# First attention of a four-mixer transformer step: scores to scaled rows one step further ahead, and the compressed branch's probabilities and V stacked over rows for one-pass products

## The reference, cut to what matters

```python
p_cmp = masked_softmax(jnp.einsum('bghtd,bngd->bghtn', qg, k_cmp), cmp_end[None, :] <= t[:, None])
o_cmp = jnp.einsum('bghtn,bngd->btghd', p_cmp.astype(v_cmp.dtype), v_cmp)
...
o = g_blk[..., 0:1] * o_cmp + g_blk[..., 1:2] * o_sel + g_blk[..., 2:3] * o_win
...
return o @ w_out
```

## Time and profile before

| | |
|---|---|
| median of 3 runs | 2051.27 us (2050.69 to 2051.84) |
| the profiled execution's own time | 2049.75 us |
| its span, first to last instruction | 2047.9 us |
| TensorE matmuls busy | 1899.2 us (93%), x8988 |
| VectorE busy | 897.6 us (44%), x1324 |
| ScalarE busy | 742.0 us (36%), x1190 |
| GpSimd busy | 820.9 us (40%), x413 |
| mean granted clock of TensorE | 0.969 |
| chain that ended last, by engine | PE 79%, DVE 9%, POOL 4%, ACT 4%, issue 4% |

### The profile page before, as it was taken

How to read it: one execution, slowest core, us unless ns; L and a number is a source line. 1 busy time by engine, 2 the same in 40 slices (tenths; PEclk the granted TensorE clock), 3 DMA queues, 4 the chain that set the end, 5 groups by cost and what they waited for, 6 DMA issues and landing times.

```text
span 2047.9 us, 24253 instructions
## 1 busy us (share of the span) xinstructions
PE 1899.2 (93%) x8988; PEld 1530.5 (75%) x8988; DVE 897.6 (44%) x1324; ACT 742.0 (36%) x1190; POOL 820.9 (40%) x413
## 2 busy tenths in 40 slices
PE   5999999899899999998999969999898999999986
PEld 3786767688788888877677448878786888888865
DVE  5136786601458824863731451126465431032116
ACT  5346776342333222223233332224322432133232
POOL 3244666363034454445233044350033344434431
PEclk9999999999999999999999779999998999999988
DMA  4321000242022233233122002320021222222221
GB/s 146 116 100 41 1 1 29 85 155 103 1 93 99 96 123 120 85 107 123 58 85 99 21 0 82 103 96 8 11 103 64 100 98 91 98 103 85 100 103 41
DMA packets 24116, 162.43 MB, mean 79 GB/s; under 512 B 2800, under 2 KB 3312, under 8 KB 4976
## 3 DMA queue, kind: packets, MB, share of 16 engines
q1 hardware_dynamic: 23040, 159.39, 22.0%
q10 hardware_dynamic: 1008, 2.12, 0.3%
HBM read 159.40 MB, written 2.10 MB: 79 GB/s over the span
## 4 chain that ended last, share of the span: by engine, by line
PE 79%; DVE 9%; POOL 4%; ACT 4%; issue 4%; DMA 0%; DVEq 0%; SPq 0%; ACTq 0%; POOLq 0%
PE psum L451 76%; POOL w_lo L2206 2%; PE psum L753 2%; ACT w_hi_r L1033 1%; POOL q_st L2242 1%; DVE tmp L1644 1%; DVE sqt L1995 1%; ACT spare L1442 1%; DVE tmp L1852 1%; DVE tmp L2158 1%; DMA ring<-in_panels 0%; DVE acc L2003 0%; DVE negmax L2050 0%; DVE h_lo L1800 0%; DVE xt L1603 0%
## 5 line engine op out<-in xcount | busy, mean ns | idle before, releaser
L2206 POOL TENSOR_TENSOR w_lo<-ring,w_hi_r 128x2048 fp32r<-128x2048 f32 x142 | 657.4, 4631 | 989.8 <-ACT w_hi_r L1033 989.7
L451 PE MATMUL psum<-big_r,w_hi_r 128*128 128x512 f32 (+1 forms) x1568 | 479.1, 389 | 33.0 <-DVE big_r L1582 8.7
L451 PE MATMUL psum<-h_hi,w_hi_r 128*128 128x512 f32 x1200 | 473.3, 394 | 20.5 <-POOL w_lo L2206 11.5
L451 PE MATMUL psum<-h_lo,w_hi_r 128*128 128x512 f32 x1200 | 469.7, 391 | 0.0
L451 PE MATMUL psum<-h_hi,w_lo 128*128 128x512 f32 x1200 | 469.4, 391 | 0.0
L1033 ACT CAST w_hi_r<-ring 128x2048 fp32r<-128x2048 f32 x144 | 274.1, 1904 | 285.6 <-PE psum L451 282.8
L451 PEld LDWEIGHTS psum<-big_r,w_hi_r 128*128 128x128 f32 x1568 | 296.9, 193 | 95.0 <-issue 32.9
L451 PE MATMUL psum<-big_r,w_lo 128*128 128x512 f32 (+1 forms) x784 | 303.5, 387 | 0.0
L451 PEld LDWEIGHTS psum<-h_hi,w_hi_r 128*128 128x128 f32 x1200 | 227.0, 189 | 74.4 <-issue 14.4
L451 PEld LDWEIGHTS psum<-h_hi,w_lo 128*128 128x128 f32 x1200 | 226.8, 189 | 47.8
L451 PEld LDWEIGHTS psum<-h_lo,w_hi_r 128*128 128x128 f32 x1200 | 227.2, 189 | 47.2 <-issue 0.5
(11 more groups left out here) (305 smaller groups left out, 2327.0 us busy)
## 6 DMA issues: line engine op xcount, KB each, us to landing
ring<-in_panels SPq DMA_DIRECT2D x148, 1024.0 KB, 4.7
xt<-in_x SPq DMA_DIRECT2D x4, 512.0 KB, 6.5
out<-big SPq DMA_DIRECT2D x8, 256.0 KB, 2.2
big<-in_mem ACTq DMA_DIRECT2D x1, 1024.0 KB, 4.6
q_st<-in_ple ACTq DMA_DIRECT2D x1, 512.0 KB, 3.4
spare<-in_w_gate ACTq DMA_DIRECT2D x1, 192.0 KB, 6.4
spare<-in_w_k ACTq DMA_DIRECT2D x1, 128.0 KB, 8.8
params<-in_params ACTq DMA_DIRECT2D x1, 114.0 KB, 4.9
```

Of the source, the lines that this page charges most:

```text
L451: return nc.tensor.matmul(o, l, r, start=start, stop=stop, **kw)
L2206: g.tensor_tensor(w_lo[:, p], ring[:, p], plain(w_hi[:, p]), ALU.subtract).then_inc(lo_done[j], 1)
```

## The change

Two things change, both in the first attention.

1. `LEAD = 4`: in step k TensorE makes the scores of part k+4, VectorE the maximum of part k+4, ScalarE exp of part k+3, VectorE its coefficient and GpSimd its scaled rows. The steps begin at -4. Transposes, high and low halves, products and joins keep their step. Buffers keep their number (4 PSUM banks for scores, 4 in `q_st`).
2. CMP's product becomes one fp32r product over 63 rows. Rows 0 to 30 of `nsa_cmp` hold the high half of the transposed probabilities (ScalarE), rows 32 to 62 the low half (VectorE, in `nsa_low`). `vcmp` holds high and low V side by side (128 columns a group), the same in rows 0 to 30 and 32 to 62. Row 31 is zero from a memset. `vcmp` moves to `rstd`, `nsa_cmp` stays in `tmp`, both through fp32r twins. CMP's shifted scores go to `hid` instead of `q_st`, so that ScalarE's exp and not VectorE's subtraction waits for the old transposes. Transposes of part w now wait for the low half of part w-2 in every case.

```diff
-        STEPS = range(-3, max(products_at) + 2)
+        LEAD = 4
+        STEPS = range(-LEAD, max(products_at) + 2)
...
                 if w >= 2:
-                    if parts[w - 2]["br"] == CMP:
-                        pe.wait_ge(ns["hi"], w - 1)
-                    else:
-                        pe.wait_ge(ns["lo"], parts[w - 2]["lows"])
+                    pe.wait_ge(ns["lo"], w - 1)
...
                 if x["br"] == CMP:
-                    pe.wait_ge(ns["hi"], x["end"] + 1)
-                    last = mm(psum[0:HD, 6 + x["u"] % 2, :], vcmp[:, x["g"] * HD:(x["g"] + 1) * HD],
-                              nsa_cmp[x["u"] % 2], False, False)
+                    rows = HALF_ROWS + NCMP
+                    pe.wait_ge(ns["lo"], x["end"] + 1)
+                    last = mm(o, vcmp[0:rows, x["g"] * P:(x["g"] + 1) * P], nsa_cmp[x["u"] % 2][0:rows], False, False)
...
-                if 0 <= k + 3 < NW:
-                    nsa_score(parts[k + 3])
+                if 0 <= k + LEAD < NW:
+                    nsa_score(parts[k + LEAD])
...
-            nc.scalar.copy(vcmp[:, :], psum[0:NCMP, 1, 0:G * HD]).then_inc(evac[1], 1)
+            act.wait_ge(ns["zero"], 1)
+            for row in (0, HALF_ROWS):
+                last = nc.scalar.copy(nsa_cmp_values(row, 0),
+                                      psum[0:NCMP, 1, 0:G * HD].rearrange("p (g d) -> p g d", d=HD))
+            last.then_inc(ns["kv_hi"], 1)
...
+                if w >= 4:
+                    act.wait_ge(ns["turned"], w - 3)
                 if part["br"] == CMP:
-                    last = nc.scalar.activation(p, p, ACT.Exp)
+                    last = nc.scalar.activation(p, nsa_shifted(part), ACT.Exp)
...
-                if 0 <= k + 2 < NW:
-                    nsa_exp(parts[k + 2])
-                    if k + 2 == NW - 1:
+                if 0 <= k + LEAD - 1 < NW:
+                    nsa_exp(parts[k + LEAD - 1])
+                    if k + LEAD - 1 == NW - 1:
                         act.dma_start(mem_raw, a["mem"]).then_inc(mem_in, 16)
...
+            V.memset(plain(tmp_tw[:, :]), 0.0)
+            V.memset(plain(rstd_tw[:, :]), 0.0).then_inc(ns["zero"], 1)
...
+            kv += 1
+            dve.wait_ge(ns["kv_hi"], kv)
+            for row in (0, HALF_ROWS):
+                last = V.tensor_tensor(nsa_cmp_values(row, 1),
+                                       psum[0:NCMP, 1, 0:G * HD].rearrange("p (g d) -> p g d", d=HD),
+                                       nsa_cmp_values(0, 0, raw=True), ALU.subtract)
+            last.then_inc(evac[1], 1)
...
+                if part["br"] == CMP:
+                    x = nsa_cmp[part["u"] % 2]
+                    V.tensor_tensor(x[HALF_ROWS:HALF_ROWS + NCMP], psum[0:NCMP, 4 + w % 2, :], plain(x[0:NCMP]),
+                                    ALU.subtract).then_inc(ns["lo"], 1)
+                    return
...
-                    if w >= 4:
-                        dve.wait_ge(ns["turned"], w - 3)
-                    ins = V.tensor_tensor(nsa_probs(part).rearrange("p (x k) -> p x k", k=nk), s_,
+                    ins = V.tensor_tensor(nsa_shifted(part).rearrange("p (x k) -> p x k", k=nk), s_,
...
-                if 0 <= k - 1 < NW and parts[k - 1]["br"] != CMP:
+                if 0 <= k - 1 < NW:
                     nsa_low(parts[k - 1])
-                if 0 <= k + 3 < NW:
-                    nsa_max(parts[k + 3])
-                if 0 <= k + 2 < NW:
-                    nsa_coef(parts[k + 2])
+                if 0 <= k + LEAD < NW:
+                    nsa_max(parts[k + LEAD])
+                if 0 <= k + LEAD - 1 < NW:
+                    nsa_coef(parts[k + LEAD - 1])
...
-                if 0 <= k + 2 < NW:
-                    nsa_scale(parts[k + 2])
+                if 0 <= k + LEAD - 1 < NW:
+                    nsa_scale(parts[k + LEAD - 1])
```

More of the change, by code:

```diff
@@ L151, in nsa_schedule @@
             sums.append(dict(unit, br=br, first=br == SEL, last=br == WIN, blocks=blocks_, end=len(parts) - 1))
[L152 to L155, removed]
     at = {}
@@ L220, in program @@
         sqt = sb("sqt", [P, S])
-        rstd = sb("rstd", [P, S])
+        rstd, rstd_tw = sb("rstd", [P, S], twin=True)
         r_row = rstd
         gains = sb("gains", [P, 2 * KD])
-        tmp = sb("tmp", [P, 2 * S])
+        tmp, tmp_tw = sb("tmp", [P, 2 * S], twin=True)
         o_acc = sb("o_acc", [P, 2 * S])
@@ L229, in program @@
         kcmp = sb("kcmp", [P, CMPW])
-        vcmp = sb("vcmp", [NCMP, G * HD])
         spare, spare_r = sb("spare", [P, 8 * S], twin=True)
@@ L348, in nsa_probs, with nsa_shifted @@
             return q_st[:, n:n + part["nh"] * part["nk"]]
+        def nsa_shifted(part):
+            return hid[:, part["u"] % 4 * CMPW:(part["u"] % 4 + 1) * CMPW]
         def small(buf, part):
@@ L353, in small, with nsa_cmp_values @@
             return buf[:, n:n + part["nh"]]
-        nsa_cmp = [view("nsa_cmp", [NCMP, S], tmp, n * S) for n in range(2)]
+        HALF_ROWS = 32
+        vcmp = rstd_tw
+        nsa_cmp = [view("nsa_cmp", [P, S], tmp_tw, n * S) for n in range(2)]
+        def nsa_cmp_values(row, low, raw=False):
+            x = vcmp[row:row + NCMP]
+            return (plain(x) if raw else x).rearrange("p (g r d) -> p g r d", r=2, d=HD)[:, :, low, :]
         nsa_corr = [view("nsa_corr", [HD, S], buf) for buf in (acc, sqt)]
@@ L391, in program @@
         ns = {n: sem("nsa_" + n) for n in (
-            "kv_hi", "gates", "scores", "negmax", "probs", "coef", "scaled", "turned", "hi", "lo", "summed", "corr",
+            "kv_hi", "zero", "gates", "scores", "negmax", "probs", "coef", "scaled", "turned", "hi", "lo", "summed", "corr",
             "o", "o_hi", "o_lo")}
@@ L762, in nsa_product @@
                 if x["br"] == CMP:
-                    pe.wait_ge(ns["hi"], x["end"] + 1)
-                    last = mm(psum[0:HD, 6 + x["u"] % 2, :], vcmp[:, x["g"] * HD:(x["g"] + 1) * HD],
-                              nsa_cmp[x["u"] % 2], False, False)
+                    rows = HALF_ROWS + NCMP
+                    pe.wait_ge(ns["lo"], x["end"] + 1)
+                    last = mm(o, vcmp[0:rows, x["g"] * P:(x["g"] + 1) * P], nsa_cmp[x["u"] % 2][0:rows], False, False)
                 else:
                     if kt == 0:
-                        pe.wait_ge(ns["lo"], parts[x["end"]]["lows"])
+                        pe.wait_ge(ns["lo"], x["end"] + 1)
                     v = nsa_value(kt, x["br"], x["g"])
@@ L1239, in nsa_exp @@
                 p = nsa_probs(part)
+                if w >= 4:
+                    act.wait_ge(ns["turned"], w - 3)
                 if part["br"] == CMP:
-                    last = nc.scalar.activation(p, p, ACT.Exp)
+                    last = nc.scalar.activation(p, nsa_shifted(part), ACT.Exp)
                 else:
-                    if w >= 4:
-                        act.wait_ge(ns["turned"], w - 3)
                     s_ = nsa_scores(part)
@@ L1258, in nsa_hi @@
                 if part["br"] == CMP:
-                    ins = nc.scalar.copy(nsa_cmp[part["u"] % 2], psum[0:NCMP, 4 + w % 2, :])
+                    ins = nc.scalar.copy(nsa_cmp[part["u"] % 2][0:NCMP], psum[0:NCMP, 4 + w % 2, :])
                 else:
```

## The result

| | before | after |
|---|---|---|
| median of 6 runs each | 2050.98 us (2046.11 to 2051.94) | 2031.93 us (2027.29 to 2035.58) |
| ratio | | 0.9907 [0.9895, 0.992] |
| profiled execution, own time | 2049.75 us | 2029.03 us |
| its span | 2047.9 us | 2027.3 us |
| first attention, first scores to output projection | 166.01 to 347.75 = 181.74 us | 165.81 to 330.88 = 165.07 us |

The change was also timed twice more beside the kernel before, on other occasions: 2032.55 against 2049.37, and 2034.63 against 2050.3, so 16.8 and 15.7 us. The stage gives 16.67 us of this, and it does so in every profile of the change (165.07, 165.07 and 165.06 us).

A forecast was written before the change was run, and what follows sets the result against it. The prediction took TensorE to bound the kernel, with VectorE the nearest other engine. Its terms, 11.9 + 5.1 - 1.0 + 0.9 + 1.6 = 18.5 us, came off 2051.27 to give 2032.8 us, range 2027.7 to 2040.5.

The forecast's parts named there:

- product, 14 in the middle: Compressed products outside the tail: one fp32r product takes 0.48 us where 1.33 was, saving 14 x 0.85 = 11.9 us.
- lookahead, middle: Between head and tail: LEAD 4 removes 5.1 of 6.9 us of TensorE's waits for GpSimd's scaled rows; bounds 0 and 6.9.
- VectorE's 16 low halves: Compressed parts: the new low halves on VectorE mostly fall where it waits, costing 1.0 us; bounds 0 and 9.8.
- head: Start of the first attention: compressed scores fill TensorE's 3.09 us wait for the first scaled rows, gaining 0.9 us.
- tail: From the transposes at 341.17 to the output projection: 1.6 us saved of 6.58, bounds 0.5 and 1.9.
- Hence no term for it: Compressed product: its weight load runs beside the matmul ahead, so nothing was charged for it.
- the weight load of the new product is not hidden: Rival at the compressed product: 16 x 0.19 = 3.0 us lost again, 2035.8 us; chance 0.07.
- a VectorE wait at the change to the second pair of heads: Where the second pair of heads begins: TensorE still waits 1.8 us for VectorE's low half, taken off the lookahead's 6.9.
- my two cases: Head: clock falls as before, 0.9 us gained; or stays at 2.4 GHz, 3.2 gained, a rival of 2030.5 us, chance 0.30.
- The fall is seen once: Head: the clock fell once, after 3.1 us of idle, and stayed at 1.00 after weight-load idles of 1.1 and 1.6.
- One step ahead, these are gone before: Tail: with the lookahead, the last exponentials are done before ScalarE copies part 101; part of the 1.6 us saving.
- Preparation: Ahead of the attention: two memsets (1.5 us) and the V halves vanish in VectorE's idle time; cost zero.

The follow-up runs named there:

- e1: The change with the old plain fp32 compressed product, so only the lookahead of four steps is new against the kernel before; 2034.87 us, ratio 0.9928.
- e3: The change with the compressed product over all 128 rows in place of 63, the added rows zero; 2031.88 us, ratio 0.9912 against the kernel before.
- e4: The change with VectorE's compressed low half made twice, the second into rows the product does not read; 2037.84 us.
- e7: e3 plus eight fill matmuls in TensorE's idle 1.8 us ahead of the first compressed scores; 2030.14 us, ratio 0.9904 against the kernel before.
- e2: The change with LEAD set back to 3, so only the new compressed product is new against the kernel before; 2039.98 us, ratio 0.9949.
- e8: The change as it is, timed again beside e7 on the same chip; 2032.55 us, ratio 0.9912 against the kernel before.
- e10: The change as it is, timed again beside e9; 2034.63 us, ratio 0.9921 against the kernel before.
- e9: e7 plus ScalarE's copy of part 100 moved ahead of the last exponentials in the tail; 2028.49 us, ratio 0.9892 against the kernel before.
- e5: The change with the compressed product over 64 rows, and again over 96, in place of 63; 2030.92 us with 64, 2031.59 us with 96.

## Why the prediction was right, by its own steps

| term | forecast | measured in the stage |
|---|---|---|
| product, 14 in the middle | 11.9 | 14 x (1.33 - 0.75) = 8.1 |
| lookahead, middle | 5.1 | 6.6 (e1) |
| VectorE's 16 low halves | -1.0 | 7.1 - 8.1 = -1.0 (what is missing from e1 to the change) |
| head | 0.9 | 2.0 |
| tail | 1.6 | 0.9 |
| sum | 18.5 | 16.7 |

The forecast of 2032.8 us stands 0.9 us above the median of 2031.93, and nearer than its parts deserve. Four terms missed (by -3.8, +1.5, +1.1 and -0.7 us), and the errors largely cancelled, to -1.8 us in the stage. Some 2.4 us that came from outside the stage, for which the forecast had nothing, made up for these. The closeness is luck; what held is that both halves work, that nothing of the preparation shows and that VectorE's new work is cheap.

- **The product was mis-sized by 3.8 us.** The step that failed is "Hence no term for it": that the new product's weight load runs beside the matmul ahead. I argued from loads of 128 rows between products of 128 rows, and carried it over to 63. The rival "the weight load of the new product is not hidden", given 0.07, is what happened, and it was too small (3.0 us for 16), because the load behind the product is exposed too (0.42 to the next start where I had 0.24). As for the Trainium skill's rule named in the prediction (loads overlap only where row groups differ), e3 goes against its "only": loads of 128 rows between matmuls of 128 rows are hidden. (The same section also lets through a load into a background weight buffer, which the prediction left out.) The rule's result, a load that shows, came true for 63 rows, and there the change of mode, above, is the rule that tells the four heights apart.
- **The lookahead gave 6.6, not 5.1.** I left 1.8 us as a VectorE wait at the change to the second pair of heads. It is there, but smaller: 0.63 us in e1 (transposes at 261.65), 0.90 in the change. The change's timeline at this place:

```profile
256.22 0.68 DVE L1851 TENSOR_TENSOR o_acc<-psum,sqt 64x512 f32<-64x512 f32 x1
...
256.94 0.69 DVE L1823 TENSOR_TENSOR h_lo<-psum,h_hi 128x512 fp32r<-128x512 f32 x1
...
257.77 0.60 PE L758 MATMUL psum<-ident,q_st 128*31 128x128 f32 x4 [0.90 <-DVE h_lo L1823]
```

  A join and the low half behind it hold the transposes for 0.90 us, as the working said; the rest of the count on VectorE did not come to bear. GpSimd's scaled rows for the same transposes were done at 257.26, the low half at 257.63.
- **VectorE's low halves cost 1.0, as forecast,** between bounds of 0 and 9.8, but not where I put it. From e1 to the change the middle falls by 7.14 where the products alone give 8.1. Compared start by start, the two traces show four places where TensorE's transposes come later against the rest, and they make up 0.84 us: 0.24 at 218.14 (the low half ends at 218.00), 0.27 at 257.77, 0.23 at 297.65, and 0.10 at 179.50, which may still belong to the head. Elsewhere the starts show no cost of it. The working had 0.1 in each of the eight long units, so the sum is right by luck. The new instruction takes what the earlier trace rows said, 0.68 us, on 31 rows as on 128. That it stayed cheap is a matter of the room on VectorE: e4 shows that the next such half costs 6.0 us.
- **The head gave 2.0, between my two cases.** I had the clock either falling as before (0.9) or staying up (3.2). It fell, but for half as long: low from 172.4 to 175.8 us instead of 172.6 to 179.4. Neither case foresaw this. ("The fall is seen once" holds for the stage alone: the trace before has two more falls within 200 us behind it, at 397.9 and 541.2 us.) And e7, where it stays up, shows that 3.2 was not to be had: 2.5 in all.
- **The tail gave 0.9 of 1.6.** "One step ahead, these are gone before" failed: the copy of part 101 (326.60) is clear of the last part's exponentials (324.03 to 325.41), but these now stand in front of the copy of part 100, whose transposes are done at 324.4, and its low half holds the transposes of part 102 (326.84, above). The two shorter products, counted there, give nothing by themselves (e2: 6.57 against 6.58).
- **Preparation:** nothing, as forecast. The projection of the keys starts at 100.05 us against 100.19.
- **What the text had not:** 3.8 us of the profiled difference, from behind the stage. The same work 190 us behind the end of the stage, first before, then after:

```profile
538.00:548.00 10.00, 6.84 (x20) 5.18 (x19) 2.62 (x5) 1.17 (x2) 0.00 (x0) 0.66 0.00 0
```

```profile
521.00:531.00 10.00, 6.84 (x34) 5.39 (x33) 2.75 (x5) 1.17 (x2) 0.00 (x0) 1.00 0.00 0
```

  The clock falls there in one execution and not in the other. e8 and e10, the change itself, have the fall (clock 0.93 in both from 150 to 200 us behind the stage; 1.00 in the first profile). Over the whole stretch behind the stage, (1 - clock) x length is 60 us before, 55 in the first profile of the change and 60 in its two others, with 1696.4 us behind the stage for 55, and 1699.8 and 1699.7 for 60. Why it falls in some executions only stays open.

Of what the prediction said would be seen, one matmul per unit and a VectorE near 90% (94%) held. The waits for scaled rows are 2.7 us and not under 2, the stage 16.7 us shorter and not 18, TensorE's busy time down by 16.5 and not 12. "A loading gap ahead of the new product" had been named as a sign of error, and it is there.

## What to carry to other kernels

A matmul of 63 or 64 rows among matmuls of 128 cost a gap on either side of it here (0.29 us in all); padded with zero rows to 96 or 128 it cost none. A deeper lookahead removes waits for a slow producer, and how much it gives is read where the next engine has slack, so count that engine's instructions before adding to it. Where one engine's order is changed, the engines behind it need the same change, or the wait moves to them, as in e9.

## What the runs showed of the hardware

- Adding rows made a matmul cheaper: 63 and 64 rows 0.75 us from the product ahead to the one behind, 96 and 128 rows 0.47 and 0.46. The load itself takes 0.18 to 0.19 us in all of them (e3, e5).
- A low half on 31 partitions takes 0.68 us, like one on 128 (0.69).
- In the change the granted clock fell to 1.2 GHz at 172.4 us, 1.1 us after the end of an idle time of TensorE of 1.8 us (and one of 1.0 us before that), stayed there 3.4 us, and did not fall where the 1.8 us were filled (e7, e9). Before, it fell at the end of an idle time of 3.0 us and stayed there 6.8 us.
- One kernel's executions differ by 3.4 us behind the stage, with clock falls that come in one and not in another, while the stage repeats to 0.1 us.
